# Narrower down products, wider first iterations and no repeated matmuls in the feed-forward blocks of a float32 transformer kernel

## The chip, the core and the metric

The kernel runs on one core of one Trainium2 chip. The metric is the device time of one execution in microseconds; the times shown are of three runs, and one further execution was profiled. TensorE multiplies a 128x128 block of weights (the stationary operand, loaded by an LDWEIGHTS) with up to 512 columns of a moving operand and adds the result up in PSUM, which has eight banks of 512 float32 values per partition.

## What is computed

The program is two transformer blocks in float32, one after the other. There are five feed-forward blocks (FFNs), numbered 0 to 4; 0 and 1 work on 528 tokens (512 and 16 meta tokens), 2, 3 and 4 on 512. Between them stand a pooling mixer, a latent attention, and a second block with three branches (attention, convolution, short convolution) and their gates.

```python
D_MODEL = 1024; D_FF = 2816; SEQ = 512; N_META = 16

def swiglu(h, w_gate, w_up, w_down):
    return (jax.nn.silu(h @ w_gate) * (h @ w_up)) @ w_down

# first block, layers l = 0, 1 (FFNs 0 and 1, then 2 and 3)
h = h + 0.5 * swiglu(rmsnorm(h, ffn1_norm[l]), ffn1_w_gate[l], ffn1_w_up[l], ffn1_w_down[l])
...                                    # pooling mixer or latent attention
h = h + 0.5 * swiglu(rmsnorm(h, ffn2_norm[l]), ffn2_w_gate[l], ffn2_w_up[l], ffn2_w_down[l])
...
# second block (FFN 4)
hf = rms_norm(x, ffn_norm_g[l]) @ w_ffn_in[l]
gt, up = jnp.split(hf, 2, axis=-1)
x = x + (jax.nn.silu(gt) * up) @ w_ffn_out[l]
```

## The kernel before

Every product is made in three matmuls. Weights and activations are split into a high part (rounded for TensorE's fast float32 format) and a low part (the rest): wH and wL, xH and xL or aH and aL. A product is wH x xH, wH x xL, wL x xH, in this order, into the same place in PSUM. Each matmul loads its own weights first. Activations are stored transposed, features on partitions and tokens along the columns.

Weights come in units of 128x1024, loaded by SyncE's queue into raw (6 buffers), turned into wH and wL (rings of 5 slots) by ScalarE, VectorE and, for a part of the low halves, an adding DMA issued by GpSimd. TensorE's program waits for a unit in weights(u), line 682.

PSUM is used as four slots of two banks each; ps[:, 2 * s] and ps[:, 2 * s + 1] are the banks of slot s. A slot is given by group(), line 659, which waits until its last reader is done.

An FFN (line 769) is cut into four parts, PAIRS = (2, 3, 3, 3): parts of the hidden features, two 128-blocks per iteration. For each part TensorE first runs the gate and up products (stage "gu", part 0 to 3), then the down products of that part (stage "dn").

- The first iteration of part 0 is first_iteration(f), line 728: plain products g1, g2, u1, u2, each over four k-blocks and two output blocks j, made as two matmuls per operand pair, one for each half of the tokens, into the two banks of a slot (line 760). In FFNs 3 and 4 the statistics product of the norm (line 709, a full-precision float32 matmul of ones with the sums of squares) stands behind the first output block of g2, which is 72 of the 192 matmuls. In FFN 2 a statistics product stands ahead of the first iteration, and another, for the latent norm, 48 matmuls before the end of part 0.
- All other iterations are seven units of products (of sums of halves; turns, line 118) of 2 x 4 x 3 = 24 matmuls with half the tokens, 256 columns for the 512-token FFNs (line 816). There are 168 in part 0 and 504 in each of the parts 1 to 3.
- At line 814 the variable again makes the first matmul of unit 2 in the last iteration of the parts 1 and 2 twice, in FFNs 2, 3 and 4. It is a starting matmul (start=True), so the second overwrites the first.
- The down products: n units for each half dg of the eight output blocks, and for each unit four output blocks d and two hidden blocks fl. product(), line 669, makes one: three matmuls over all tokens, 512 columns into one bank for the 512-token FFNs; for the 528-token ones two matmuls, of 256 and 272 columns, into two banks. A part has 96 matmuls of 512 columns (part 0) or 144 (each other). Only the last output block of FFN 4 is made in halves already, by half_product (line 689).
- At line 851, in FFNs 3 and 4 only, one extra matmul of 512 columns stands in part 0, before the second output block of dg 1; the product behind it starts afresh and overwrites it.

VectorE reads the first iteration's slots in first_gating (line 1979 on): halves(s, T) is the pair of 256-column halves of two banks; pairs(ap) is one piece of 512 columns seen as two.

Of the kernel before, what the change touches and what calls it, by code (L numbers as in the profile page):

```python
# [20 lines left out]
ALU = mybir.AluOpType  # L21
# [3 lines left out]
P = 128  # L25
# [5 lines left out]
T1 = SEQ + NMETA  # L31
# [246 lines left out]
def program(nc, w, out, C):  # L278
# [3 lines left out]
    with ctx:  # L282
# [359 lines left out]
        def _(pe):  # L642
# [23 lines left out]
                C.slot[name] = s  # L666
                return s

            def product(s, T, wcol, sl, rhs, start, stop):

                aH_, aL_ = rhs
                parts = [(0, CUT), (CUT, T1)] if T == T1 else [(0, T)]
                wh, wl = wH[:, sl, wcol:wcol + P], wL[:, sl, wcol:wcol + P]
                for n, (lhs, r) in enumerate(((wh, aH_), (wh, aL_), (wl, aH_))):
                    for c, (a, b) in enumerate(parts):
                        to = CUT if T == T1 and c == 0 else 0
                        ins = nc.tensor.matmul(ps[:, 2 * s + c, to:to + b - a], lhs, r[:, a:b],  # L677
                                               start=start and n == 0, stop=stop and n == 2,
                                               skip_group_check=True)
                return ins  # L680

# [46 lines left out]
            def first_iteration(f):  # L728
# [15 lines left out]
                for p, only in runs:  # L744
# [4 lines left out]
                    for j, k in ([(j, k) for k in range(KP) for j in range(2)] if p == "g1" else  # L749
# [6 lines left out]
                        c = k * 2 * P + j * P  # L756
                        wh, wl = (t[:, (U0[st] + i) % RING, c:c + P] for t in (wH, wL))
                        for q, (lhs, x) in enumerate(((wh, bH), (wh, bL), (wl, bH))):
                            for half in range(2):
                                ins = nc.tensor.matmul(ps[:, 2 * s + half, 0:TH], lhs, x[:, b + half, k, :],  # L760
                                                       start=e == k == q == 0,
                                                       stop=e == 1 and k == KP - 1 and q == 2,
                                                       skip_group_check=True)
# [5 lines left out]
            def ffn(f):  # L769
# [5 lines left out]
                for part, n in enumerate(PAIRS):  # L775
                    st = f"gu{f}{part}"
                    for it in range(n):
# [6 lines left out]
                        for i, p in enumerate(turns(part, it)):  # L784
# [18 lines left out]
                            for j in range(2):  # L803
                                if p == 4:
                                    pe.wait_ge(dve_done, at("dve", f"{st}:{it}:u22{j}"))
                                for k in range(KP):
                                    if part == 0 and it == 1 and j == 0 and p in (4, 5, 6, 7):
                                        pe.wait_ge(dve_done, at("dve", f"x{p}:f{f}:{k}"))
                                    c = k * 2 * P + j * P
                                    wh, wl = (t[:, (u + i) % RING, c:c + P] for t in (wH, wL))  # L810
                                    xh, xl = (t[:, XI[p], k, :] for t in (bH, bL))
                                    for q, (lhs, rhs) in enumerate(((wh, xh), (wh, xl), (wl, xh))):
                                        begin = p in (1, 5, 2) and k == q == 0
                                        again = f > 1 and 0 < part < 3 and begin and p == 2 and it == n - 1 and j == 0
                                        for _ in range(1 + again):
                                            ins = nc.tensor.matmul(ps[:, 2 * s + j, 0:TH], lhs, rhs, start=begin,  # L816
                                                                   stop=p in (2, 3, 4) and k == KP - 1 and q == 2,
                                                                   skip_group_check=True)
                                done(ins, f"{st}:{it}:{p}.{j}")
                            if f == 2 and part == 0 and it == 1 and p == 3:  # L820
                                borrow("kv", T1, 3 - x, f"ss:kv:{KKV - 1}")
# [3 lines left out]
                    for dg in range(2):  # L825
                        sl = []

                        for js in down_steps(n, dg, part):
                            for j in js:
                                weights(u + dg * n + j)  # L830
                            for d in range(4):
# [14 lines left out]
                                for fl in range(2 * js[0], 2 * js[-1] + 2):  # L846
                                    j, e = fl // 2, fl % 2
                                    if dg == 0 and d == 0 and e == 0:
                                        pe.wait_ge(dve_done, at("dve", f"gu{f}{part}:{j}:lo"))
                                    if f > 2 and part == 0 and dg == 1 and d == 1 and fl == 0:  # L850
                                        nc.tensor.matmul(ps[:, 2 * sl[d], 0:T], wH[:, (u + n) % RING, d * P:d * P + P],
                                                         aH[:, 0, :], start=True, stop=False,
                                                         skip_group_check=True)
                                    ins = product(sl[d], T, e * 512 + d * P, (u + dg * n + j) % RING,
                                                  (aH[:, fl, :], aL[:, fl, :]),
                                                  fl == 0, fl == 2 * n - 1)
                                if js[-1] == n - 1:
                                    done(ins, f"{st}:{4 * dg + d}")
                            if js[-1] < n - 1:
# [919 lines left out]
        def _(dve):  # L1779
# [199 lines left out]
            def first_gating(f, gain):  # L1979
# [2 lines left out]
                name = f"{st}:0"  # L1982
                r = norm(f).rearrange("p (c n) -> p c n", c=2)

                def gates():
                    for j in range(2):
                        on_pe(f"{name}:g2.{j}")
                        do(V.tensor_tensor(pairs(t1[:, j, 0:T]), halves(C.slot.get(f"{name}:g{j}", 0), T), r, ALU.mult),
                           f"rd:{name}:g{j}", f"{name}:g{j}")

                def ups():
                    for j in range(2):
                        on_pe(f"{name}:u2.{j}")
                        on_act(f"{name}:silu{j}")
                        do(V.scalar_tensor_tensor(pairs(m[:, j, 0:T]), halves(C.slot.get(f"{name}:u{j}", 0), T), -1.0,
                                                  pairs(t2[:, j, 0:T]), ALU.mult, ALU.mult),
                           f"rd:{name}:u{j}", *([f"{name}:m"] if j else []))

# [709 lines left out]
```

## Time and profile before

| | |
|---|---|
| median of the runs | 2399.51 us (3 runs, 2398.27 to 2400.09) |
| the profiled execution, first to last instruction | 2396.0 us |
| TensorE busy | 2387.8 us, 16268 matmuls |
| TensorE weight loads busy | 2193.6 us |
| VectorE busy | 1566.9 us |
| ScalarE busy | 1452.6 us |
| matmuls at line 816, 256 columns, each operand pair | 1680 to 1686, mean 277 ns |
| matmuls at line 677, 512 columns (aH, aL), each operand pair | 522, mean 389 to 394 ns |
| DMA | 401.37 MB, mean 168 GB/s |

A matmul's duration is longer than its distance from the next one, because matmuls are pipelined; the distance is read from a stretch's length over its count. PE is TensorE, PEld its weight loads, DVE VectorE, ACT ScalarE, POOL GpSimd, SP SyncE.

### The profile page before, as it was taken

What the parts mean: (1) busy time and instruction counts of PE and PEld (TensorE: products, weight loads), DVE (VectorE), ACT (ScalarE), POOL (GpSimd) and SP (SyncE); (2) the same over time, 40 slices, a digit from 0 to 9 for tenths busy, and PEclk for the clock granted to TensorE, in tenths of its full rate; (3) what the DMA queues carried; (4) which work ended last, traced back from release to release, by engine and by line L of the source; (5) the groups of instructions that cost most, each with busy time, mean ns of one, the idle gap of its engine ahead of it and who ended that gap; (6) DMA issues with size and microseconds to landing.
All of it is one profiled execution on the core that took longest, in us unless ns stands there. A gap on an engine that the chain in (4) does not pass through costs nothing.

```text
span 2396.0 us, 40147 instructions
## 1 busy us (share of the span) xinstructions
PE 2387.8 (100%) x16268; PEld 2193.6 (92%) x16268; DVE 1566.9 (65%) x2190; ACT 1452.6 (61%) x1914; POOL 281.3 (12%) x330
## 2 busy tenths in 40 slices
PE   9999999999999999999999999999999999999999
PEld 9999999999999999998689999977778888999998
DVE  8756656867565867675778576654786533776664
ACT  7547466554476575477775564766875565654743
POOL 0101010110011010011001110111011111110101
DMA  7658594685588486688346776986556888575866
GB/s 217 162 141 204 146 225 95 150 221 124 141 203 212 124 207 162 159 208 208 77 89 173 197 168 160 233 186 145 123 125 162 189 186 192 130 180 156 206 159 155
DMA packets 244345, 401.37 MB, mean 168 GB/s; under 512 B 12304, under 2 KB 170896, under 8 KB 244160
## 3 DMA queue, kind: packets, MB, share of 16 engines
q0 software_dynamic: 46944, 170.94, 38.9%
q1 hardware_dynamic: 197216, 227.85, 29.7%
q8 instruction: 130, 2.13, 0.4%
q14 instruction: 55, 0.45, 0.1%
HBM read 225.73 MB, written 2.10 MB: 95 GB/s over the span
## 4 chain that ended last, share of the span: by engine, by line
PE 97%; DVE 1%; DMA 1%; ACT 1%; issue 0%; SPq 0%; DVEq 0%; ACTq 0%
PE ps L677 45%; PE ps L816 40%; PE ps L760 4%; PE ps L1150 1%; PE ps L1186 1%; PE ps L1174 1%; PE ps L1195 1%; PE ps L1062 1%; PE ps L1026 1%; PE ps L1046 1%; PE ps L886 1%; PE ps L865 0%; DMA raw<-in_ffn_w_up 0%; PE ps L917 0%; PE ps L709 0%
## 5 line engine op out<-in xcount | busy, mean ns | idle before, releaser
L816 PE MATMUL ps<-xbH,wH 128*128 128x256 f32 (+1 forms) x2806 | 784.2, 280 | 0.6 <-DMA wL<-raw 0.5
L816 PE MATMUL ps<-xbL,wH 128*128 128x256 f32 (+1 forms) x2800 | 782.3, 279 | 0.0
L816 PE MATMUL ps<-xbH,wL 128*128 128x256 f32 (+1 forms) x2800 | 782.3, 279 | 0.0
L816 PEld LDWEIGHTS ps<-xbH,wH 128*128 128x128 f32 x2806 | 526.5, 188 | 1.4 <-issue 0.6
L816 PEld LDWEIGHTS ps<-xbL,wH 128*128 128x128 f32 x2800 | 526.2, 188 | 0.4
L635 POOL DMA_DIRECT2D wL<-raw x326 | 281.1, 863 | 2086.6 <-ACT wL L1272 2067.9
L816 PEld LDWEIGHTS ps<-xbH,wL 128*128 128x128 f32 x2800 | 525.6, 188 | 0.0
L1272 ACT ACTIVATE wL<-raw 128x1024 fp32r<-128x1024 f32 x326 | 343.8, 1055 | 174.0 <-PE ps L677 131.5
L1290 ACT ACTIVATE wH<-raw 128x1024 fp32r<-128x1024 f32 x375 | 392.5, 1048 | 79.4 <-PE ps L677 50.9
L1286 ACT ACTIVATE wH<-wS 128x1024 fp32r<-128x1024 f32 x200 | 212.0, 1060 | 344.9 <-DVE wS L1825 327.2
L677 PE MATMUL ps<-aH,wL 128*128 128x256 f32 (+1 forms) x1226 | 348.9, 331 | 0.0
L677 PE MATMUL ps<-aH,wH 128*128 128x256 f32 (+1 forms) x1226 | 346.6, 329 | 0.4 <-DVE aL L1976 0.2
L677 PE MATMUL ps<-aL,wH 128*128 128x256 f32 (+1 forms) x1226 | 346.8, 329 | 0.0
L1834 DVE TENSOR_TENSOR wL<-wS,wH 128x1024 fp32r<-128x1024 f32 x200 | 243.9, 1219 | 1.3 <-ACT wH L1286 0.2
L677 PEld LDWEIGHTS ps<-aL,wH 128*128 128x128 f32 x1226 | 208.6, 188 | 22.2
L677 PEld LDWEIGHTS ps<-aH,wH 128*128 128x128 f32 x1226 | 208.6, 188 | 22.2 <-issue 0.9
L677 PEld LDWEIGHTS ps<-aH,wL 128*128 128x128 f32 x1226 | 208.0, 188 | 19.8
L1825 DVE TENSOR_TENSOR wS<-raw 128x1024 f32<-128x1024 f32 x100 | 122.1, 1221 | 114.6 <-PE ps L816 114.6
L677 PE MATMUL ps<-xH,wH 128*128 128x512 f32 (+1 forms) x488 | 187.8, 393 | 0.0
L677 PE MATMUL ps<-xH,wL 128*128 128x512 f32 (+1 forms) x488 | 182.3, 382 | 0.0
L677 PE MATMUL ps<-xL,wH 128*128 128x512 f32 (+1 forms) x488 | 182.1, 381 | 0.0
L1825 DVE TENSOR_TENSOR wS<-wS,raw 128x1024 f32<-128x1024 f32 x100 | 122.1, 1221 | 57.8 <-PE ps L677 48.0
(316 smaller groups left out, 3228.0 us busy)
## 6 DMA issues: line engine op xcount, KB each, us to landing
wL<-raw POOLq DMA_DIRECT2D x326, 512.0 KB, 5.6
raw<-in_ffn_w_gate SPq DMA_DIRECT2D x88, 512.0 KB, 5.3
raw<-in_ffn_w_up SPq DMA_DIRECT2D x88, 512.0 KB, 6.0
raw<-in_ffn_w_down SPq DMA_DIRECT2D x88, 512.0 KB, 5.4
raw<-in_w_in SPq DMA_DIRECT2D x56, 512.0 KB, 4.3
raw<-in_w_ffn_in SPq DMA_DIRECT2D x44, 512.0 KB, 5.4
raw<-in_w_ffn_out SPq DMA_DIRECT2D x22, 512.0 KB, 5.4
raw<-in_w_o SPq DMA_DIRECT2D x12, 512.0 KB, 5.5
```

What stands on the lines that cost most here:

```text
L635: nc.gpsimd.dma_start(wL[:, u % RING, :], raw[:, UNITS[u].raw % RAW, :], accum_op=ALU.add).then_inc(lo_in[u % RING], 16)
L677: ins = nc.tensor.matmul(ps[:, 2 * s + c, to:to + b - a], lhs, r[:, a:b], start=start and n == 0, stop=stop and n == 2, skip_group_check=True)
L760: ins = nc.tensor.matmul(ps[:, 2 * s + half, 0:TH], lhs, x[:, b + half, k, :], start=e == k == q == 0, stop=e == 1 and k == KP - 1 and q == 2,
L816: ins = nc.tensor.matmul(ps[:, 2 * s + j, 0:TH], lhs, rhs, start=begin, stop=p in (2, 3, 4) and k == KP - 1 and q == 2, skip_group_check=True)
L886: ins = nc.tensor.matmul(ps[:, 2 * sl[t] + g // 2, g % 2 * 2 * P:(g % 2 + 1) * 2 * P], lhs, r, start=a == 0 and n == 0, stop=a == 1 and n ...
L1026: ins = nc.tensor.matmul(b0, lhs, r[:, k, 0:SEQ], start=k == n == 0, stop=k == KQ - 1 and n == 2, skip_group_check=True)
L1046: ins = nc.tensor.matmul(b0[:, 0:n], q, kcat[:, hd, 0:n], start=True, stop=True)
L1272: nc.scalar.activation(wL[:, s, :], raw[:, r % RAW, :], ACT.Copy, scale=-1.0).then_inc(n_done, 1)
L1286: nc.scalar.activation(wH[:, s, :], wS[:, s, :], ACT.Copy).then_inc(h_done, 1)
L1290: nc.scalar.activation(wH[:, s, :], raw[:, r % RAW, :], ACT.Copy).then_inc(h_done, 1)
L1825: do(V.tensor_tensor(wS[:, u % RING, :], a, b, ALU.add), f"sum:{u}")
L1834: do(V.tensor_tensor(wL[:, s, :], a, f32(wH[:, s, :]), ALU.subtract), f"low:{u}")
```

## The change

It concerns FFNs 2, 3 and 4, those of 512 tokens.

- Down products are made in two matmuls of 256 columns per operand pair, into the two halves of the same bank, first half then second, with the same weights loaded for each. The first unit's two products of output block 0 in each part (6 matmuls) stay at 512 columns. Only the first half of a starting product carries start=True.
- The first iteration's matmuls take both halves of the tokens at once: 512 columns (the moving operand lies in two pieces of 256) into one bank. VectorE reads them from there.
- The repeated matmul in the parts 1 and 2 (again) and the extra one in part 0 of FFNs 3 and 4 are left out.

```diff
--- before.py
+++ after.py
@@ -666,16 +666,18 @@
                 C.slot[name] = s
                 return s
 
-            def product(s, T, wcol, sl, rhs, start, stop):
+            def product(s, T, wcol, sl, rhs, start, stop, halved=False):
 
                 aH_, aL_ = rhs
                 parts = [(0, CUT), (CUT, T1)] if T == T1 else [(0, T)]
+                if halved:
+                    parts = [(0, T // 2), (T // 2, T)]
                 wh, wl = wH[:, sl, wcol:wcol + P], wL[:, sl, wcol:wcol + P]
                 for n, (lhs, r) in enumerate(((wh, aH_), (wh, aL_), (wl, aH_))):
                     for c, (a, b) in enumerate(parts):
-                        to = CUT if T == T1 and c == 0 else 0
-                        ins = nc.tensor.matmul(ps[:, 2 * s + c, to:to + b - a], lhs, r[:, a:b],
-                                               start=start and n == 0, stop=stop and n == 2,
+                        bank, to = (0, a) if halved else (c, CUT if T == T1 and c == 0 else 0)
+                        ins = nc.tensor.matmul(ps[:, 2 * s + bank, to:to + b - a], lhs, r[:, a:b],
+                                               start=start and n == 0 and not (halved and c), stop=stop and n == 2,
                                                skip_group_check=True)
                 return ins
 
@@ -756,6 +758,12 @@
                         c = k * 2 * P + j * P
                         wh, wl = (t[:, (U0[st] + i) % RING, c:c + P] for t in (wH, wL))
                         for q, (lhs, x) in enumerate(((wh, bH), (wh, bL), (wl, bH))):
+                            if f > 1:
+                                ins = nc.tensor.matmul(pairs(ps[:, 2 * s, 0:T]), lhs, x[:, b:b + 2, k, :],
+                                                       start=e == k == q == 0,
+                                                       stop=e == 1 and k == KP - 1 and q == 2,
+                                                       skip_group_check=True)
+                                continue
                             for half in range(2):
                                 ins = nc.tensor.matmul(ps[:, 2 * s + half, 0:TH], lhs, x[:, b + half, k, :],
                                                        start=e == k == q == 0,
@@ -811,11 +819,9 @@
                                     xh, xl = (t[:, XI[p], k, :] for t in (bH, bL))
                                     for q, (lhs, rhs) in enumerate(((wh, xh), (wh, xl), (wl, xh))):
                                         begin = p in (1, 5, 2) and k == q == 0
-                                        again = f > 1 and 0 < part < 3 and begin and p == 2 and it == n - 1 and j == 0
-                                        for _ in range(1 + again):
-                                            ins = nc.tensor.matmul(ps[:, 2 * s + j, 0:TH], lhs, rhs, start=begin,
-                                                                   stop=p in (2, 3, 4) and k == KP - 1 and q == 2,
-                                                                   skip_group_check=True)
+                                        ins = nc.tensor.matmul(ps[:, 2 * s + j, 0:TH], lhs, rhs, start=begin,
+                                                               stop=p in (2, 3, 4) and k == KP - 1 and q == 2,
+                                                               skip_group_check=True)
                                 done(ins, f"{st}:{it}:{p}.{j}")
                             if f == 2 and part == 0 and it == 1 and p == 3:
                                 borrow("kv", T1, 3 - x, f"ss:kv:{KKV - 1}")
@@ -847,13 +853,9 @@
                                     j, e = fl // 2, fl % 2
                                     if dg == 0 and d == 0 and e == 0:
                                         pe.wait_ge(dve_done, at("dve", f"gu{f}{part}:{j}:lo"))
-                                    if f > 2 and part == 0 and dg == 1 and d == 1 and fl == 0:
-                                        nc.tensor.matmul(ps[:, 2 * sl[d], 0:T], wH[:, (u + n) % RING, d * P:d * P + P],
-                                                         aH[:, 0, :], start=True, stop=False,
-                                                         skip_group_check=True)
                                     ins = product(sl[d], T, e * 512 + d * P, (u + dg * n + j) % RING,
-                                                  (aH[:, fl, :], aL[:, fl, :]),
-                                                  fl == 0, fl == 2 * n - 1)
+                                                  (aH[:, fl, :], aL[:, fl, :]), fl == 0, fl == 2 * n - 1,
+                                                  f > 1 and (dg, d, fl // 2) != (0, 0, 0))
                                 if js[-1] == n - 1:
                                     done(ins, f"{st}:{4 * dg + d}")
                             if js[-1] < n - 1:
@@ -1982,17 +1984,21 @@
                 name = f"{st}:0"
                 r = norm(f).rearrange("p (c n) -> p c n", c=2)
 
+                def both(what):
+                    s = C.slot.get(f"{name}:{what}", 0)
+                    return halves(s, T) if f < 2 else pairs(ps[:, 2 * s, 0:T])
+
                 def gates():
                     for j in range(2):
                         on_pe(f"{name}:g2.{j}")
-                        do(V.tensor_tensor(pairs(t1[:, j, 0:T]), halves(C.slot.get(f"{name}:g{j}", 0), T), r, ALU.mult),
+                        do(V.tensor_tensor(pairs(t1[:, j, 0:T]), both(f"g{j}"), r, ALU.mult),
                            f"rd:{name}:g{j}", f"{name}:g{j}")
 
                 def ups():
                     for j in range(2):
                         on_pe(f"{name}:u2.{j}")
                         on_act(f"{name}:silu{j}")
-                        do(V.scalar_tensor_tensor(pairs(m[:, j, 0:T]), halves(C.slot.get(f"{name}:u{j}", 0), T), -1.0,
+                        do(V.scalar_tensor_tensor(pairs(m[:, j, 0:T]), both(f"u{j}"), -1.0,
                                                   pairs(t2[:, j, 0:T]), ALU.mult, ALU.mult),
                            f"rd:{name}:u{j}", *([f"{name}:m"] if j else []))
 
```

## Rows read from the trace of the kernel before

**Rows 1.** The page's head and its first line of part 1.

```profile
span 2396.0 us, 40147 instructions
...
PE 2387.8 (100%) x16268; PEld 2193.6 (92%) x16268; DVE 1566.9 (65%) x2190; ACT 1452.6 (61%) x1914; POOL 281.3 (12%) x330
```

**Rows 2.** TensorE's waits, whole span: us in total, times, longest.

```profile
PE ps L738 <- DMA gains<-in_gains: 3.1, 1, 3.1
PE ps L865 <- ACT t L1594: 0.7, 2, 0.5
```

**Rows 3.** Windows: busy of each engine, granted clock, DMA share, GB/s.

```profile
900.00:1000.00 100.00, 100.00 (x694) 92.32 (x693) 71.11 (x86) 54.95 (x62) 10.35 (x12) 1.00 0.73 188
```

**Rows 4.** Chain of work, FFN 2: start us, us, what, count.

```profile
768.64 22.61 PE ps L760 x192
...
891.15 32.96 PE ps L677 x144
924.11 57.23 PE ps L816 x505
```

**Rows 5.** Chain of work, FFNs 3 and 4 (from 2055).

```profile
1228.19 8.48 PE ps L760 x72
...
1237.53 14.13 PE ps L760 x120
1251.66 19.79 PE ps L816 x168
...
2055.56 8.16 PE ps L760 x72
...
2120.70 59.48 PE ps L816 x505
```

**Rows 6.** TensorE groups by shape, 892 to 923: count, busy us, mean ns.

```profile
L677 PE MATMUL ps<-aL,wH 128*128 128x512 f32 x46 | 18.0, 392 | 0.0
L677 PE MATMUL ps<-aH,wH 128*128 128x512 f32 x46 | 17.8, 388 | 0.0
L677 PE MATMUL ps<-aH,wL 128*128 128x512 f32 x45 | 17.7, 394 | 0.0
```

**Rows 7.** The same, 2111.2 to 2120.4, then 2122 to 2179.

```profile
L677 PE MATMUL ps<-aH,wL 128*128 128x512 f32 x14 | 5.5, 392 | 0.0
...
L816 PE MATMUL ps<-xbH,wH 128*128 128x256 f32 x163 | 45.3, 279 | 0.0
```

**Rows 8.** The same, 1212.5 to 1227.9 (w_o), then 1228.2 to 1236.3.

```profile
L677 PE MATMUL ps<-oH,wL 128*128 128x512 f32 x23 | 8.9, 388 | 0.0
...
L760 PE MATMUL ps<-xbL,wH 128*128 128x256 f32 x24 | 4.8, 280 | 0.0
```

**Rows 9.** The same around statistics: 1830-1893, 1897-1910; 1916-2000; 1085-1114, 1117-1121.

```profile
L677 PE MATMUL ps<-xH,wL 128*128 128x512 f32 x62 | 24.1, 388 | 0.0
...
L677 PE MATMUL ps<-xH,wL 128*128 128x512 f32 x14 | 5.5, 392 | 0.0
...
L677 PE MATMUL ps<-xH,wL 128*128 128x512 f32 x83 | 32.7, 394 | 0.0
...
L677 PE MATMUL ps<-xH,wL 128*128 128x512 f32 x14 | 5.5, 394 | 0.0
...
L677 PE MATMUL ps<-xH,wL 128*128 128x512 f32 x6 | 2.4, 392 | 0.0
```

**Rows 10.** Line 677, 1271 to 1272; groups 1272.4 to 1283.8; 1284.2 to 1293.7.

```profile
L677 PE MATMUL ps<-aH,wH x1: 476/476/476, 1271.5 to 1271.5; 128*128 128x512 f32 x1
...
L677 PE MATMUL ps<-aH,wL 128*128 128x512 f32 x18 | 7.1, 392 | 0.0
...
L677 PE MATMUL ps<-aH,wL 128*128 128x512 f32 x14 | 5.5, 394 | 0.0
```

**Rows 11.** Groups by shape, 2012 to 2055 (w_o2), then 2099 to 2110.6.

```profile
L677 PE MATMUL ps<-mgH,wL 128*128 128x512 f32 x63 | 24.8, 394 | 0.0
...
L677 PE MATMUL ps<-aH,wL 128*128 128x512 f32 x18 | 7.0, 388 | 0.0
```

**Rows 12.** Groups by shape, 813.5 to 833.5, then 2182 to 2212.8.

```profile
L677 PE MATMUL ps<-aH,wL 128*128 128x512 f32 x29 | 11.4, 394 | 0.0
...
L677 PE MATMUL ps<-aH,wL 128*128 128x512 f32 x46 | 18.1, 394 | 0.0
```

## Prediction

> **What bounds the kernel now.** I read the page first, then the table by windows, then the chain of work, then TensorE's groups by shape. The page [rows 1] shows TensorE busy for 2387.8 of 2396.0 us; the longest wait that the list of TensorE's waits names is 3.1 us, at the start, and all of the others are 0.7 or less in total [rows 2]. The windows [rows 3] show the full granted clock, so every stretch has the higher of the two levels, 2.4 GHz. So the end is set by how closely products follow one another on TensorE, and nothing else has to be followed unless it comes to hold TensorE up. The profiled execution spans 2396.0 us; the median of the runs is 2399.51, 3.5 us more, and I add those 3.5 at the end.
>
> The chain gives the spacing as length over count [rows 4, 5]. Down products of 512 columns: 32.96 us / 144 = 228.9 ns, so 686.7 ns for one product (three matmuls: high x high, high x low, low x high). Gate and up products of 256 columns: 57.23 / 505 = 113.3 ns in most parts, but 59.48 / 505 = 117.8 ns in part 1 of the last FFN, and 19.79 / 168 = 117.8 in part 0 of FFNs 3 and 4. It is the same code. The first iteration's 256-column matmuls show both spacings too: 8.16 / 72 = 113.3 ahead of the statistics product of FFN 4 and 14.13 / 120 = 117.8 behind it. So a 256-column stream has two rhythms, tight (113.3) and loose (117.8), and each lasts for hundreds of matmuls, across banks, operands and unit boundaries.
>
> **What chooses the rhythm.** The mean durations by operand pair show it. In a stretch of 512-column products the three matmuls take 388, 392 and 394 ns in turn; which operand pair has which value stays for the whole stretch [rows 6]. Where the low-weight one (aH,wL), the last of every product, has 394, the 256-column stream behind it is tight: the stretch from 891.15 is one, and part 2 follows it at 113.3. Where it has 392, as ahead of the 59.48 us part of FFN 4 [rows 7], or 388, as ahead of FFN 3 [rows 8], that stream is loose. I found no boundary without a stall that goes against this. In a loose stream the values rotate with period 3 as well. Every count in this kernel (a product, a unit of 24, a part) is a multiple of three, so a rhythm, once entered, repeats itself. Only two things rotate it: a statistics product (full-precision, not a triple) or a stall, and the single extra matmuls that the change removes. For the statistics products the table is: the low-weight matmul at 388 before gives 392 after, 392 gives 394, 394 gives 392 [rows 9], each seen once.
>
> **The change part by part.**
> (a) Halving. The three 512-token FFNs have 3 x 176 = 528 down products; six come as half products already, and two in each of 12 parts stay whole. That leaves 498 products, 1494 matmuls that become 2988. In the tight rhythm six of 256 columns take 6 x 113.3 = 680.0 ns against 686.7: -6.7 ns a product, -3.3 us in all. In the loose one 6 x 117.8 = 706.7: +20.0 ns, +10.0 us in all. No row shows two halves into one bank with the same weights; the two nearest are the part-1 rows (one bank, new weights) and the first iteration's 72 (two banks in turn, the same weights loaded for both), and both have 113.3 when tight, so I take these and no extra. The weight loads double in number: L816's rate already carries one load per 113.3 ns.
> (b) First iterations: 3 x 192 matmuls of 256 columns become 3 x 96 of 512, 96 x 228.9 = 21.97 us each. Before they take 22.61, 8.48 + 14.13 = 22.61 and 8.16 + 14.13 = 22.29 [rows 4, 5]: -0.64, -0.64, -0.32. Their moving operand now lies in two pieces, which no row has at this size; I take zero, with the spread of 512-column spacing on either side (96 x 4.5 ns = 0.4 us each).
> (c) Extra matmuls: six of 256 columns and two of 512 go, 0.23 us in FFN 2, 0.46 in FFN 3, 0.35 in FFN 4 (0.12 + 0.23).
> (d) VectorE reads one bank instead of two halves, equal elements; it has idle time beside every part [rows 3] and its two readers are off the chain: nothing. Some 2400 more instructions are fetched, 6% of 40147 [rows 1], and L816's stream is fed at the denser rate already: nothing.
> (e) The rhythms. This is the large term. A part of 504 matmuls costs 504 x 4.45 = 2.24 us more when loose.
>
> FFN 2. Nothing ahead of it changes. Its part 0 is loose now up to the second statistics product, and 48 matmuls behind that the first down product starts a stretch that ends with 394 [rows 12]. The first iteration and 120 matmuls lie between the two statistics products; their count stays a multiple of three, so I keep the same exit. Result: tight, as now: 168 x -6.7 = -1.12, -0.64, -0.23 = -2.0 us.
>
> FFN 3. The w_o products ahead end with the low-weight one at 388 [rows 8]; 36 matmuls (12 whole products) keep that, the statistics product turns it to 392 (first line of the table), and 60 more keep 392. So part 0 stays loose, 168 matmuls. At its end there is a short stall (the first down matmul shows 476 ns), and the down products behind it settle with the low-weight matmul at 392: the window of that row begins with the fifth matmul, so the sixth is one of them. Before, the extra matmul of dg 1 turned this to 394 in time for part 1 [rows 10]; it is gone. So the six whole matmuls end in 392, the halved stream starts loose, and since all counts are multiples of three it stays loose to the end of the FFN: 1512 x 4.45 = +6.73, 168 x 20.0 = +3.36, -0.64, -0.46 = +9.0 us.
>
> FFN 4. The w_o2 products end in 394 [rows 11]; the statistics product turns this to 392 (third line of the table). Part 0 is loose. It leaves at another point of the cycle than now, when it left at 388 and the extra matmul made it 392, loose either way [rows 7, 11]. Which value six whole matmuls reach from the new point no row shows without a stall; FFN 3 left its loose stream from this point, with the stall, and got 392. I take that. Then parts 2 and 3, tight now, become loose: 1008 x 4.45 = +4.48; 162 x 20.0 = +3.24; the 36 half-product matmuls +0.16; -0.32; -0.35: +7.2 us.
>
> Sum: -2.0 + 9.0 + 7.2 = +14.2; 2396.0 + 14.2 = 2410.2, and with the 3.5 us around it 2413.7.
>
> A rule of the Trainium skill bears on (a): "TensorE: Matmul & The Clock Gate", section "Back-to-back issue gap", gives a gap of N/2.4 + 2.5 ns. An estimate from it is 2.5 ns more for each matmul cut in two: +3.7 us for 1494, -0.7 for the 288 joined in (b). The trace disagrees: two of 256 take 226.7 or 235.6 ns against 228.9 for one of 512. What a fixed cost for each matmul would do here is rival F.
>
> **The rivals.**
> B, all three FFNs tight. The six whole matmuls are then enough to bring the stream into the tight rhythm from wherever it is. For it: in FFN 2 and in part 1 of FFN 4 a whole stretch of 512 columns that follows a loose stream does end in 394 [rows 12]. Against it: FFN 3's stretch did not, before its extra matmul. FFN 2 -2.0; FFN 3 -1.12 - 0.64 - 0.46 = -2.2; FFN 4 loses its loose part 1: -2.24 - 1.08 - 0.32 - 0.35 = -4.0. Sum -8.2, time 2391.3; with part 0 tight as well up to 1.5 less. This is faster, the other side, and decided by one thing: whether the sixth matmul in FFNs 3 and 4 has 394.
> C, just one FFN locked loose. FFN 2 locked would be 6.73 + 3.36 - 0.64 - 0.23 = +9.2. Any one of the three gives -2.0 + 9.0 - 4.0 = +3.0 (or the same to 0.1): 2402.5.
> D, all locked: 9.2 + 9.0 + 7.2 = +25.4, 2424.9.
> E, the change doesn't do what it says: halves that share a bank never run tight, whatever the neighbours do. Then 498 x 20.0 = +10.0, -1.6 - 1.1: +7.3, 2406.8.
> F, each matmul carries a fixed cost beside its columns. From the 512-column row that would be 228.9 - 512/2.4 = 15.6 ns; six of 256 would take 6 x (106.7 + 15.6) = 733.6, +46.9 ns a product, +23.4 - 1.6 - 1.0 = +20.8 us, 2420.3. The rows at 113.3 speak against it.
>
> **How the numbers follow.** My forecast A 0.37: FFN 3's row is direct but a stall may land elsewhere in the cycle, FFN 4's step is by analogy, and the table has one row for each line. B 0.29, C 0.21, D 0.05, E 0.06, F 0.02. About 0.2% (4.8 us) is what a measurement can tell from no change: A, D, E and F are slower, C is the same, B faster: 0.50, 0.21, 0.29. The likeliest case's own range is 2410 to 2417 (the 0.4 us of each first iteration, the runs' 1.8 us). The range for all reaches from B to A, 2389 to 2418, and leaves out D and F.
>
> **What would show it.** The after-trace's L816 duration in each part (276 or 280), and the low-weight matmul's duration among the first six of each dn stretch: 394 where the rest is tight, 392 or 388 where it is loose. The halved stream should show 276 or 279/280 and nothing else; 282 or more would be E. The first iterations should take 22.0 us each. If a dn stretch of FFN 3 begins with 392 and its halves still show 276, the rule by which I chose the state is wrong. If FFN 2's part 1 is loose, the step "same exit" failed. If any TensorE wait of over 1 us appears, (d) failed.

## The result

The changed kernel takes 2410.36 us in the median of eight runs (2395.77 to 2412.96), the kernel before 2398.89 in eight beside them (2396.06 to 2404.72). The ratio is 1.0031, with a 95% interval of 1.0017 to 1.0045: slower, by a little more than what can be told from no change. On a second occasion, with five runs of the changed kernel beside eleven of the other, it was 1.0050 (1.0038 to 1.0062). The profiled execution spans 2411.1 us and took 2412.89; the prediction had 2410.2 for the span and 2413.7 for the time. Among the runs of all the kernels below, one, of the kernel called seven, took 4818 us; it is left out of that kernel's ratio.

The page's head and TensorE's line, kernel after:

```profile
span 2411.1 us, 42543 instructions
...
PE 2401.7 (100%) x17466; PEld 2256.9 (94%) x17466; DVE 1567.5 (65%) x2190; ACT 1453.5 (60%) x1914; POOL 281.1 (12%) x330
```

Nothing but TensorE has changed against [rows 1]: VectorE, ScalarE and GpSimd are busy as long as before, and TensorE is still busy throughout. So the 15.1 us lie in the spacing of its matmuls. The chain of work, kernel after (start us, us, what, count), FFNs 2, 3 and 4:

```profile
769.12 21.99 PE ps L762 x96
...
833.57 57.12 PE ps L822 x504
890.69 32.65 PE ps L679 x282
...
1226.68 8.24 PE ps L762 x36
...
1235.78 13.74 PE ps L762 x60
1249.53 19.79 PE ps L822 x168
1269.31 0.19 issue
1269.50 22.83 PE ps L679 x186
1292.33 59.39 PE ps L822 x504
1351.73 33.88 PE ps L679 x282
...
2063.28 8.24 PE ps L762 x36
...
2128.75 59.36 PE ps L822 x504
```

Lines 760, 816 and 677 of the kernel before are 762, 822 and 679 here. In FFN 2 a part of 504 takes 57.12 us, 113.3 ns each, as in [rows 4]; the down products of a part take 32.65 us where they took 32.96. In FFNs 3 and 4 the same instructions take 59.36 to 59.39 (117.8 ns each) and 33.88 us. These two FFNs were to stay loose, and every part of both is.

Between the statistics products that end FFNs 2 and 3, these are the boundaries in the kernel before (its chain) and then in the one after:

```profile
1115.37 0.86 PE ps L709 x2
...
1575.37 1.72 PE ps L709 x4
```

```profile
1113.88 0.86 PE ps L711 x2
...
1583.07 1.72 PE ps L711 x4
```

FFN 2, from its first iteration to that product: 1115.37 - 768.64 = 346.73 before, 1113.88 - 769.12 = 344.76 after, -2.0 us (forecast -2.0). FFN 3: 1575.37 - 1228.19 = 347.18 and 1583.07 - 1226.68 = 356.39, +9.2 (forecast +9.0). FFN 4, from its first iteration (2055.56 [rows 5] and 2063.28) to the end of the span: 340.44 and 347.82, +7.4 (forecast +7.2). The rest of the 15.1 is that FFN 2 starts 0.5 us later; the stretches between the FFNs agree to 0.02 us.

The groups by shape show the cycle at each of the predicted points, kernel after. FFN 3: the w_o products (1208.9 to 1226), the 60 matmuls behind the statistics (1236.4 to 1249), the sixth whole matmul (window 1270.6 to 1270.9), the halves (1271.3 to 1292):

```profile
L679 PE MATMUL ps<-oH,wL 128*128 128x512 f32 x25 | 9.7, 389 | 0.0
...
L762 PE MATMUL ps<-xbH,wL 128*128 128x512 f32 x19 | 7.5, 392 | 0.0
...
L679 PE MATMUL ps<-aH,wL 128*128 128x512 f32 x1 | 0.4, 393 | 0.0
...
L679 PE MATMUL ps<-aL,wH 128*128 128x256 f32 x60 | 11.9, 279 | 0.0
```

FFN 4: behind the statistics (2072.5 to 2085.7), the sixth whole matmul of part 0 (2107.0 to 2107.3), and of part 1 (2189.0 to 2189.32), where no stall stands in between; then the halves of FFN 2 (813.4 to 833):

```profile
L762 PE MATMUL ps<-xbH,wL 128*128 128x512 f32 x19 | 7.5, 392 | 0.0
...
L679 PE MATMUL ps<-aH,wL 128*128 128x512 f32 x1 | 0.4, 392 | 0.0
...
L679 PE MATMUL ps<-aH,wL 128*128 128x512 f32 x1 | 0.4, 392 | 0.0
...
L679 PE MATMUL ps<-aL,wH 128*128 128x256 f32 x59 | 11.6, 276 | 0.0
```

The low-weight matmul goes from 389 over 392 to 393 in FFN 3 and from 392 to 392 in FFN 4: loose both times, and FFN 2's halves are tight at 276 ns. Single durations differ by up to 1 ns from one cycle to the next, so 389 is the place of 388 and 393 that of 392.

One thing in FFN 3 wasn't forecast. A loose 256-column stream has a cycle of three too: one operand pair lasts 280 ns, the other two 279. In part 1 of FFN 3 the 280 stands at one pair before 1312 and at another behind it (windows 1296 to 1311.5 and 1313 to 1340):

```profile
L822 PE MATMUL ps<-xbL,wH 128*128 128x256 f32 x45 | 12.6, 280 | 0.0
...
L822 PE MATMUL ps<-xbH,wL 128*128 128x256 f32 x77 | 21.6, 280 | 0.0
```

Between them, at 1312.11, a matmul starts 147 ns after the one before it, 29 ns late. The down products of part 1 then end their six whole matmuls in 389, not in 392. Both leave the FFN loose; had the cycle moved to the other place, it would have become tight from there.

### The profile page after: what moved, and what is told of

It reads as the page before. It is cut to its first block, busy times and chain, and to the rows that moved or that the text cites. A ratio compares the mean times of both kernels' runs of the same rounds, so it can differ in the third digit from the quotient of the medians.

```text
span 2411.1 us, 42543 instructions
## 1 busy us (share of the span) xinstructions
PE 2401.7 (100%) x17466; PEld 2256.9 (94%) x17466; DVE 1567.5 (65%) x2190; ACT 1453.5 (60%) x1914; POOL 281.1 (12%) x330
## 4 chain that ended last, share of the span: by engine, by line
PE 97%; DVE 1%; DMA 1%; ACT 1%; issue 0%; SPq 0%; DVEq 0%; ACTq 0%
PE ps L679 45%; PE ps L822 40%; PE ps L762 3%; PE ps L768 1%; PE ps L1152 1%; PE ps L1188 1%; PE ps L1176 1%; PE ps L1197 1%; PE ps L1064 1%; PE ps L1028 1%; PE ps L1048 1%; PE ps L888 1%; PE ps L867 0%; DMA raw<-in_ffn_w_up 0%; PE ps L919 0%; PE ps L711 0%
## 5 line engine op out<-in xcount | busy, mean ns | idle before, releaser
L679 PEld LDWEIGHTS ps<-aH,wH 128*128 128x128 f32 x1724 | 267.4, 188 | 2.7 <-issue 1.2
L679 PEld LDWEIGHTS ps<-aL,wH 128*128 128x128 f32 x1724 | 266.8, 188 | 0.5
L679 PEld LDWEIGHTS ps<-aH,wL 128*128 128x128 f32 x1724 | 265.9, 188 | 1.0
```

The source lines that it names most:

```text
L679: ins = nc.tensor.matmul(ps[:, 2 * s + bank, to:to + b - a], lhs, r[:, a:b], start=start and n == 0 and not (halved and c), stop=stop and ...
```

## The experiments

Theory 1 is that of the prediction: where in the cycle of 388, 392 and 394 ns the last 512-column matmul stands decides the rhythm of the 256-column stream behind it. Rival 1: halves in one bank are costly by themselves. Rival 2: six whole matmuls are too few, and more of them bring the tight rhythm.

**One more whole matmul where it should help.** Before the first down product of part 0 in FFNs 3 and 4, its first matmul is made once more than needed; the product overwrites it.

```diff
+if f > 2 and part == dg == d == fl == 0:
+    for _ in range(1):
+        nc.tensor.matmul(ps[:, 2 * sl[d], 0:T], wH[:, u % RING, 0:P],
+                         aH[:, 0, :], start=True, stop=False, skip_group_check=True)
```

> The changed kernel with one more whole matmul ahead of the first down product of part 0 in FFNs 3 and 4 (a copy of that product's first matmul, which then overwrites it): seven 512-column matmuls instead of six. Theory 1, the order in the cycle of 388, 392 and 394 ns decides: the matmul ahead of the first half then has 394 in place of 392, and both FFNs run tight (276 ns) from there on. Each gains 1512 x 4.45 + 168 (or 162) x 26.7 ns = 11.2 us over the changed kernel, less 0.23: about 22 us in all, span about 2389. Rival, halves in one bank bring the loose rhythm by themselves: no change, span 2411.

Measured: median 2393.47 us of ten runs, ratio to the kernel before 0.9978 (0.9957 to 0.9999). The profiled one spans 2392.4, 3.4 more than forecast: it has two stalls in tight streams (below). It was run again beside the changed kernel on one chip:

> The kernel called seven once more, beside the changed kernel: 15 to 20 us less than that in the median (both FFNs tight from part 0's down products on), and less than the kernel before by 4 to 7 us. If what made it short was the chip of its first call, it is within 5 us of the changed kernel.

> The changed kernel as it is, beside the next three on one chip. Theory 1: a median near 2410, with single runs down to 2396 where a stall happens to bring FFN 3 or FFN 4 back to the tight rhythm; its distances in steps of about 2.2 us, one part of gate and up products.

Measured: the changed kernel 2411.85 (2407.34 to 2413.54), ratio 1.0050 (1.0038 to 1.0062); with the seventh matmul 2390.71 (2390.46 to 2397.60), ratio 0.9970 (0.9957 to 0.9983). One matmul of 0.23 us in each of two FFNs takes 21.1 us off the changed kernel (forecast 15 to 20) and leaves it 7.8 us below the kernel before (forecast 4 to 7). The span is 2388.7, forecast 2389. The chain of seven_2 in FFN 3, at part 0 and its down products:

```profile
1249.14 19.79 PE ps L822 x168
1268.93 0.14 issue
1269.55 21.79 PE ps L679 x186
```

Its groups by shape, halves of FFN 3 (1270.8 to 1291):

```profile
L679 PE MATMUL ps<-aH,wH 128*128 128x256 f32 x60 | 11.7, 276 | 0.0
```

Part 0 ahead of it is loose as before (19.79 us), the stall is there too (0.14), and from the first half on it is tight: 21.79 us in place of 22.83. (The seventh whole matmul has a line of its own and isn't in these 186.) Rival 1 is out, since these are the same halves in the same banks.

**Two more, and a third whole product.** The first has range(2) in the edit above. The second keeps the cycle and adds three matmuls:

```diff
-f > 1 and (dg, d, fl // 2) != (0, 0, 0))
+f > 1 and (dg, d, fl // 2) != (0, 0, 0) and (dg, d, fl) != (0, 1, 0))
```

> The same with two more whole matmuls, eight in all. Theory 1: the matmul ahead of the first half has 388, the halves run loose (279 and 280 ns), and both FFNs stay so: span about 2411. Rival 2, the more whole matmuls stand first, the surer the tight rhythm: as with seven, about 2389.

> The changed kernel with three whole products (nine matmuls) first in each part in place of two. Theory 1: nine is six and three, so nothing turns: 392 ahead of the first half in FFNs 3 and 4, loose, FFN 2 tight: span about 2411. Rival 2, more whole matmuls help: about 2389.

Measured: eight has a median of 2409.35 (2391.76 to 2413.72) and a span of 2411.9, forecast 2411; nine has 2405.96 (2391.48 to 2414.10) and 2406.0, 5 us less than forecast. Their ratios are 1.0024 (1.0000 to 1.0048) and 1.0019 (1.0001 to 1.0038). Groups by shape, eight, FFN 3 from 1270.8 on:

```profile
L679 PE MATMUL ps<-aH,wL 128*128 128x512 f32 x1 | 0.4, 388 | 0.0
...
L679 PE MATMUL ps<-aH,wH 128*128 128x256 f32 x56 | 11.1, 279 | 0.0
```

The same of nine, from 1275 on:

```profile
L679 PE MATMUL ps<-aL,wH 128*128 128x256 f32 x54 | 10.7, 279 | 0.0
```

With six the last is 392 or 393, with seven the halves are tight, with eight the last is 388 and they are loose, with nine they are loose. More is not better; the remainder by three counts. Rival 2 is out.

In two places the count alone doesn't give the value. In FFN 4 of eight the last whole matmul of part 0 has 392 and not 388 (window 2107.8 to 2108.1), and in FFN 4 of seven_ffn2 (below), where nothing was edited, the sixth has 388 and not 392:

```profile
L679 PE MATMUL ps<-aH,wL 128*128 128x512 f32 x1 | 0.4, 392 | 0.0
```

Both are loose either way, so no time shows it. At both boundaries there is the short stall at the end of part 0; what it does is counted in the next section.

Nine's shorter span comes from FFN 4, where a stall in part 1 brought it back to the tight rhythm from part 1's down products on; a stall in FFN 2 did the opposite (below).

**The same seventh matmul where it should harm.** In FFN 2, which is tight without it:

```diff
-if f > 2 and part == dg == d == fl == 0:
+if f == 2 and part == dg == d == fl == 0:
```

> The changed kernel with the seventh whole matmul in part 0 of FFN 2 alone, the FFN that runs tight from there. Theory 1, the order in the cycle decides and not the number of whole matmuls: FFN 2's whole stretch now ends in 388, its halves and the parts 1 to 3 run loose (278 to 281 ns): 1512 x 4.45 + 168 x 26.7 ns = +11.2 us on the changed kernel, span 2422 where FFNs 3 and 4 are as there. Rival 2, a seventh whole matmul helps anywhere: 2411.

Measured: median 2422.42 (2412.05 to 2423.26), ratio 1.0086 (1.0068 to 1.0104), span 2421.5, forecast 2422. Its chain in FFN 2:

```profile
811.41 22.58 PE ps L679 x186
833.98 59.36 PE ps L822 x504
```

Its groups by shape, the two whole products behind the extra matmul (811.5 to 812.7), their low-weight matmuls:

```profile
L679 PE MATMUL ps<-aH,wL 128*128 128x512 f32 x2 | 0.8, 388 | 0.0
```

394 has become 388, and all of FFN 2 is loose. The same edit is worth -21 us where it is made in FFNs 3 and 4 and +11 where it is made in FFN 2.

**The repeated 256-column matmuls put back.** They stand in the parts 1 and 2 of each of the three FFNs.

```diff
+again = f > 1 and 0 < part < 3 and begin and p == 2 and it == n - 1 and j == 0
+for _ in range(1 + again):
```

> The changed kernel with the repeated 256-column matmul of the parts 1 and 2 put back (six matmuls), the extra 512-column one still out. Theory 1: FFNs 3 and 4 stay loose in part 0's down products and part 1's gate and up products; the repeat turns the cycle by one there, the six whole matmuls of part 1's down products end in 394, and all behind is tight. A tight stream isn't turned by it. Each of the two FFNs gains 1008 x 4.45 + (138 or 132) x 26.7 ns = 8.2 us over the changed kernel: span about 2395. If the repeats do nothing: 2412.

Measured: median 2402.94 (2398.08 to 2409.84), ratio 1.0009 (0.9996 to 1.0021), span 2400.9, forecast 2395. The chain, parts 1 and 2 of FFN 3, then part 2 of FFN 4:

```profile
1291.60 59.48 PE ps L824 x505
1351.08 32.67 PE ps L679 x282
1383.74 57.23 PE ps L824 x505
...
2212.34 58.84 PE ps L824 x505
```

In FFN 3 it is as forecast: part 1 is loose, the repeat turns the cycle, and from part 1's down products on all is tight. FFN 4 does the same in part 1 (59.48 and 32.67 us), but its part 2 takes 58.84 us, and all behind it is loose to the end. Its groups by shape before and behind 2231 show why it is neither 57.2 nor 59.5:

```profile
L824 PE MATMUL ps<-xbH,wL 128*128 128x256 f32 x54 | 14.9, 276 | 0.0
...
L824 PE MATMUL ps<-xbH,wH 128*128 128x256 f32 x109 | 30.2, 279 | 0.0
```

A very short stall stands at 2231 (a matmul starts 144 ns after the one before, 31 ns late), and the tight stream is loose behind it. The prediction had named stalls as something that turns the cycle, but it counted only the one at the end of part 0 and none inside a part. Both seven and nine have such a place. In seven it is at 1311.37 of TensorE's timeline (start, us, line, tile, what it waited for):

```profile
1311.37 0.36 PE L822 MATMUL ps<-xbH,wH 128*128 128x256 f32 x1 [0.46 <-issue]
```

Seven's groups by shape show 276 ns before it (1293 to 1310.5) and 279 behind it (1312.5 to 1350).

What the stall waits for isn't named by the profile ("issue"). It comes at the first matmul of an iteration's first unit, where new weights are needed, in a stretch in which the DMA engines are taken up entirely (share 1.01 between 1304 and 1311). That the weights are late is likely, not shown: the kernel before has the same share there, 1.02 between 1306 and 1313, and no stall.

**Both extras together,** the edit of seven and that of again:

> The changed kernel with the seventh whole matmul of part 0 in FFNs 3 and 4 and with the repeated 256-column matmuls of the parts 1 and 2 as well. Theory 1 with what the runs of seven and again added (a stall inside a tight stretch leaves it loose, and the cycle then has to be turned again): the same best case as seven plus 0.7 for the repeats, span about 2391, with repeats that turn a part which a stall has made loose; so a narrower spread than seven, whose runs went up to 2412.7. Rival, the repeats don't turn anything: the spread of seven.

> The kernel called seven_again once more. If its 2402.6 us came from more stalls on the chip of its call, it is within 2 us of seven_2 now. If the repeated matmuls do harm (where a stall has left a part loose, the repeat turns the cycle away from 394 as often as towards it), it stays 5 to 9 us above.

Measured: 2402.57 (2391.94 to 2408.19), ratio 1.0004 (0.9989 to 1.0020), and the second time 2398.44 (2391.12 to 2413.89), ratio 1.0001 (0.9978 to 1.0024), while seven_2 beside it had 2390.71. The spans are 2396.5 (forecast 2391) and 2396.1. So with the repeats the kernel is some 8 us slower than without them on the same chip too; the chip of the first call isn't the reason. In both profiled executions part 2 of FFN 2 is stalled near 942 us and is loose from there to the end of the FFN. Why a stall comes there and not in seven_2 isn't settled.

What a repeat does to a loose stream can be read. In part 2 of FFN 2 of seven_again, before and behind the repeat at 975.8 (windows 968 to 975 and 976 to 980.5), the operand pair with 280 ns is:

```profile
L824 PE MATMUL ps<-xbH,wH 128*128 128x256 f32 x20 | 5.6, 280 | 0.0
...
L824 PE MATMUL ps<-xbH,wL 128*128 128x256 f32 x13 | 3.6, 280 | 0.0
```

The first of these places leads to 394 at the end of the next six whole matmuls, the second to 388 (the counts are in the next section). So here the repeat turned a stream away from the tight rhythm that the down products would otherwise have found. The profiles of the kernels that have the repeats hold 36 of them. The 22 in a tight stream change nothing. The 14 in a loose one all move the cycle by one step: six from the place of 392 to that of 394, five from 388 to 392, three from 394 to 388. A repeat helps only where the stream stands at 392, and does harm at 394. In seven_again_2 it went from 388 to 392, loose either way. So a repeat kept a stream loose in just one of the two profiles, and how much of the 8 us is the repeats' isn't settled.

**Each part of the change alone, on the kernel before.** Three edits of the kernel before: its eight extra matmuls left out; its down products halved, and nothing else; its first iterations wide, and nothing else.

```diff
-for _ in range(1 + again):
-if f > 2 and part == 0 and dg == 1 and d == 1 and fl == 0:
-    nc.tensor.matmul(ps[:, 2 * sl[d], 0:T], ...)
```

```diff
-              (aH[:, fl, :], aL[:, fl, :]), fl == 0, fl == 2 * n - 1)
+              (aH[:, fl, :], aL[:, fl, :]), fl == 0, fl == 2 * n - 1,
+              f > 1 and (dg, d, fl // 2) != (0, 0, 0))
```

```diff
+if f > 1:
+    ins = nc.tensor.matmul(pairs(ps[:, 2 * s, 0:T]), lhs, x[:, b:b + 2, k, :], ...)
+    continue
```

> The kernel before without its repeated and extra matmuls, nothing else of the change. Theory 1, their removal is what costs: FFN 3's whole stretch of 96 ends in 392 and all its parts are loose, 1512 x 4.45 = +6.7; FFN 4 leaves part 0's stretch in 388 and stays loose, parts 2 and 3 +4.5; less 1.0 for the matmuls: +10 us, span about 2406. Rival, the extra matmuls were of no use and the halving or the first iterations cost: 2396 - 1.0 = 2395.

> The kernel before with the down products halved as in the change, first iterations and extra matmuls as before. Theory 1: the extra matmuls still turn the cycle, so each FFN is tight from part 1's down products at the latest; FFN 2 -1.1; FFN 3 loose halves in part 0 +0.6, perhaps a loose part 1 +2.2, then -0.9; FFN 4 part 0 +0.6, then -0.9: between 2394 and 2398. Rival, halves in one bank cost by themselves (20 ns a product): 2406.

> The kernel before with the first iterations as in the change (512 columns into one bank), down products whole and the extra matmuls kept. Theory 1: -0.64, -0.64 and -0.32 for the first iterations; FFN 3 as before (392 turned to 394 by the extra matmul); FFN 4 now gets to the same point as FFN 3, so its extra matmul turns 392 to 394 too and its part 1 is tight, -2.24: 2396 - 3.8 = 2392. Rival, the wide first iterations turn FFN 3 the wrong way: +6.7, 2401.

Measured:

| kernel | median us (runs' lowest and highest) | ratio (95%) | span us | forecast span |
|---|---|---|---|---|
| no_extras | 2407.71 (2403.85 to 2409.04) | 1.0031 (1.0021 to 1.0041) | 2402.5 | 2406 |
| halves_only | 2408.80 (2400.65 to 2417.06) | 1.0041 (1.0025 to 1.0057) | 2401.5 | 2394 to 2398 |
| wide_first | 2407.36 (2399.54 to 2414.56) | 1.0029 (1.0012 to 1.0045) | 2410.2 | 2392 |

Leaving out eight matmuls of 1.1 us in all makes the kernel longer, by 0.31% or some 7.4 us: that much of theory 1 holds. The profiled execution of no_extras missed by 3.5 us, because the parts 1 and 2 of FFN 3, which were to be loose, are tight, while FFN 4's parts are loose. The short stall at the end of FFN 3's part 0 left its 96 whole matmuls ending in 394 and not in 392. Its chain, part 1 of FFN 3 and part 2 of FFN 4:

```profile
1294.20 57.12 PE ps L814 x504
...
2215.16 59.36 PE ps L814 x504
```

The other two missed by more, wide_first by 18 us. The first step held in halves_only, where part 1 of FFN 4 is loose and its down products tight (the first of its two fences), and in FFN 4 of wide_first, where the extra matmul made part 1 tight for its first 144 matmuls. What was missed is again the stall in a tight stream. In wide_first one stands at 852.15 and leaves FFN 2's part 1 loose from its 169th matmul on and its part 2 whole, and one at 2146.95 ends the tight stretch of FFN 4's part 1. In halves_only one stands at 1497.57 in FFN 3's part 3, and in FFN 2 part 3 is tight for 168 matmuls (19.04 / 168 = 113.3 ns), stalls at 1033.40 and goes on loose (39.81 / 336 = 118.5 ns with the stall's tail). The chain of halves_only in FFN 4, then in FFN 2:

```profile
2126.97 59.48 PE ps L818 x505
2186.44 32.67 PE ps L679 x282
```

```profile
1014.36 19.04 PE ps L818 x168
1033.40 0.14 issue
1033.53 39.81 PE ps L818 x336
```

Not every stall does this. In FFN 2 of the same execution there is one of 0.27 us, and the stream behind it stays tight, 43.88 / 385 = 114.0 ns:

```profile
847.67 0.27 issue
847.94 43.88 PE ps L818 x385
```

In wide_first it is something else in FFN 3. The down products of part 0 are in a rhythm that no stretch of [rows 6 to 12] has. Groups by shape, 1275 to 1285:

```profile
L679 PE MATMUL ps<-aH,wH 128*128 128x512 f32 x15 | 6.0, 397 | 0.0
```

Its chain at the end of part 0:

```profile
1287.08 9.80 PE ps L679 x42
1296.88 59.48 PE ps L824 x505
```

All operand pairs have 397 ns, at 9.80 / 42 = 233.3 ns for each matmul, the extra matmul turns nothing in a stream without a cycle, and the part behind is loose. It began at the same short stall ahead of the first down product. The down products behind part 1 could still have found the tight rhythm: part 1 stands at the place of 394 until its repeat, at 1350.4, moves it to that of 388. The repeat in part 1 of FFN 4, at 2183.8, does the same. Here, too, a matmul that was put in to help does harm once the stream stands elsewhere.

## Why the prediction was right, and where it was not

The forecast was a loss of 14.2 us of span through two FFNs that lock loose; it was 15.1, with FFN 2 at -2.0 as forecast, FFN 3 at +9.2 for +9.0.

(a) Halving. The two prices held: 282 matmuls of a tight part take 32.65 us (6 x 228.9 + 276 x 113.3 ns = 32.64), those of a loose one 33.88. No price of its own for a shared bank: E is out by FFN 2 and by seven_2.

(b) The first iterations take 21.99, 8.24 + 13.74 = 21.98 us each, forecast 21.97. The moving operand in two pieces costs nothing.

(c), (d) Nothing showed against them but a slip in the sum: FFN 4 loses two repeated matmuls as FFN 3 does, so its term is 0.46 and not 0.35, and its forecast +7.1 and not +7.2. TensorE's stall ahead of FFN 3's down products is 0.19 us.

(e) FFN 3 went through each step of the chain: 389, then 392, then 393 as the sixth, then 279. FFN 4's step by analogy held: 392 both with a stall (part 0) and without one (part 1). That FFN 3 then stayed loose through parts 1 to 3 isn't quite the working of the prediction: the late matmul at 1312.11 turned the cycle, and nothing in the prediction says that it had to turn to 389 and not to 394. That was luck. Seven, eight, nine and seven_ffn2 show that the place in the cycle is the cause, by moving it both ways.

The record holds more than these examples. In the 14 profiled executions there are 198 boundaries at which at least three 512-column matmuls are followed by at least forty of 256 columns. Behind a last matmul of 394 or 395 the next forty are tight in all 100 cases; behind 388, 389, 392 or 393 they are loose in all 97, and behind the one 397 too. The way into a stretch of down products without a stall is as regular, at 169 boundaries: from a tight stream the sixth whole matmul has 394 or 395 (80 of 80). From a loose stream it depends on which of the last three matmuls is the one of 280 ns: 394 or 395 with the third from the end (25 of 25), 392 with the second from the end (35 of 35), 388 or 389 with the last (29 of 29). In the gate and up products these are the operand pairs high x high, high x low and low x high. So FFN 4's step, taken by analogy, is the rule.

What isn't regular is the stall ahead of the first down product of part 0. It stands at 21 boundaries of FFNs 3 and 4, each time behind a stream at the place of 392. The sixth whole matmul then had 392 or 393 in 17, 394 in two (no_extras in FFN 3, eight in FFN 4), 388 in one and 397 in one. That the profiled execution had the likely value in both FFNs is a matter of odds, as the prediction said of FFN 3.

Rival F is out: a part's down products, 32.96 us when whole, took 32.65 tight and 33.88 loose once halved, and a fixed cost for each matmul could not give both. The formula of the Trainium skill ("TensorE: Matmul & The Clock Gate", section "Back-to-back issue gap"), N/2.4 + 2.5 ns, which the page gives for an isolated matmul, would make each matmul more cost 2.5 ns. An estimate from it is 0.35 us for the 138 more of a part, 33.31 us. These rows don't agree: 32.65 and 33.88.

What the prediction left out is the stall inside a part. It named a stall as something that turns the cycle, but took each rhythm, once entered, to repeat itself to the end of the FFN, and gave a stall inside a tight stream no term and no chance. In the 14 profiles 16 such stalls, of 25 ns or more, stand in tight 256-column streams of the three FFNs. Behind 11 the stream is loose until the next 512-column stretch, and then it depends on where in the cycle that begins; behind five it stays tight. The length doesn't decide it: 25 ns (nine, 1032.41) and 0.62 us (seven, 1311.37) turned a stream to loose, 0.09 us (halves_only, 2322.52) and 1.19 us (seven_again, 1317.42) did not. What decides it is open.

Such stalls, and the one ahead of the first down product, are likely what spreads the times: four of the eight first runs lie between 2412.47 and 2412.96, the forecast of 2413.7 less 1, and the other four at 2408.26, 2404.01, 2401.12 and 2395.77. That would also be why the median moved by 11.5 us and not by 14.2. It is an inference from the profiled executions; the record has no trace of the other runs.

A second, smaller miss is the term of 3.5 us between span and time. The profiled execution of the changed kernel took 2412.89 for a span of 2411.1: 1.8 us. The 3.5 compared the span of one execution of the kernel before with the median of others, and so took 1.7 us of their spread for overhead.

The version with the seventh matmul is shorter than both kernels, 2390.71 against 2398.48 and 2411.85 on one chip. It is rival B's time (2391.3), reached by turning the cycle.

## What to carry to other kernels

Where an engine is busy throughout, compare the spacing of the same instruction in different stretches before costing an edit by counts: here the 4% between two rhythms outweighs all that the edit saved. A matmul that computes nothing may be what brings a stream into its tight rhythm, and the same matmul can keep it out when the stream arrives at another place of the cycle (seven_again, wide_first). So when such matmuls are removed, or counts changed that aren't multiples of the period, look at the rhythm behind each place. A kernel tuned this way is sensitive to short stalls, so judge it by many runs, not by one profile.

## What the runs showed of the hardware

256-column float32 matmuls, each with its own weights, run at 113.3 or at 117.8 ns apart in unbroken stretches of up to 780, with the granted clock at 1.00 in both. 512-column ones run at 228.9 ns (388, 392 and 394 ns in turn) or, in one stretch behind a stall (wide_first), at 233.3 (397 each). A full-precision statistics product, a stall, and a single matmul more in a loose stream can each change which of these follows; a matmul that came 25 ns late was enough (nine), and stalls of up to 1.19 us sometimes changed nothing (seven_again). By the last matmul of a 512-column stretch the next 256-column stretch is tight behind 394 or 395 (100 of 100) and loose behind 388, 389, 392, 393 and 397 (98 of 98).
